# Attention scores as two stacked f32r products, with an f32r mask and separate buffers for even and odd heads

## The reference

```python
# fox: c is the running sum of the log forget gates
sc = einsum('bhqd,bhkd->bhqk', qb, k) * scale + (cb[..., :, None] - c[..., None, :])
sc = where(pos[None, :] <= tq[:, None], sc, -1e30); p = softmax(sc)
# diff: two maps c = 0, 1 for each head, one slope for each head
sc = einsum('bhcqd,bhckd->bhcqk', qb, k) * scale - slopes * (tq - pos)
p = softmax(where(pos <= tq, sc, -1e30)); a = p[:, :, 0] - lam * p[:, :, 1]
# na: 8 x 16 window clamped to the grid, bias rpb gathered by offset
sc = where(mask, einsum("bnqhd,bknjhd->bhnqkj", q_r, k_r) * scale + bias, NEG); p = softmax(sc)
```

## Time and profile before

| | us |
|---|---|
| median of three runs | 1433.59 (1426.29 to 1436.23) |
| the profiled execution's own time | 1433.59 |
| its span | 1431.8 |
| TensorE matmul busy | 1399.9 (98%) |
| TensorE weight load busy | 1137.6 |
| VectorE busy | 678.7 |
| ScalarE busy | 597.4 |
| GpSimd busy | 664.9 |

### The profile page before, as it was taken

How to read it: one execution, slowest core, us unless ns; L and a number is a source line. 1 busy time by engine, 2 the same in 40 slices (tenths; PEclk the granted TensorE clock), 3 DMA queues, 4 the chain that set the end, 5 groups by cost and what they waited for, 6 DMA issues and landing times.

```text
span 1431.8 us, 19476 instructions
## 1 busy us (share of the span) xinstructions
PE 1399.9 (98%) x6620; PEld 1137.6 (79%) x6620; DVE 678.7 (47%) x1228; ACT 597.4 (42%) x924; POOL 664.9 (46%) x886
## 2 busy tenths in 40 slices
PE   7999999999999999999998999999999999999998
PEld 5877787667888888888888777887778888888887
DVE  5566645555322222112277878666536555552111
ACT  5444433354544443334343554535335444443223
POOL 5422242215755545555545323455646545555551
PEclk9999999889999999999999999999999999999999
DMA  4321121112333333333364211332333333332331
GB/s 143 81 59 45 43 63 59 44 30 74 93 112 89 101 98 93 92 96 96 105 101 102 80 45 45 89 103 74 89 89 113 93 102 88 102 93 87 105 98 59
DMA packets 223632, 120.72 MB, mean 84 GB/s; under 512 B 15172, under 2 KB 222417, under 8 KB 223569
## 3 DMA queue, kind: packets, MB, share of 16 engines
q1 hardware_dynamic: 223569, 119.89, 29.7%
HBM read 117.56 MB, written 2.31 MB: 84 GB/s over the span
## 4 chain that ended last, share of the span: by engine, by line
PE 92%; DVE 3%; issue 1%; POOL 1%; ACT 1%; DMA 1%; SPq 1%; DVEq 0%; POOLq 0%; ACTq 0%
PE PS L677 28%; PE PS L679 27%; PE PS L678 27%; PE PS L827 2%; PE PS L838 2%; PE PS L855 2%; PE PS L828 1%; PE PS L829 1%; POOL WL L552 1%; DVE XL L1501 1%; DVE SS L1497 1%; PE PS L832 1%; DMA ROWV<-in_diff_norm_g 0%; PE PS L840 0%; SPq L451 0%
## 5 line engine op out<-in xcount | busy, mean ns | idle before, releaser
L552 POOL TENSOR_TENSOR WL<-RAW,WH 128x256 fp32r<-128x256 f32 x864 | 659.2, 795 | 735.5 <-ACT WH L1089 735.3
L677 PE MATMUL PS<-XH,WH 128*128 128x512 f32 x1088 | 434.9, 400 | 3.2 <-DVE X L1826 1.8
L679 PE MATMUL PS<-XH,WL 128*128 128x512 f32 x1088 | 425.2, 391 | 0.0
L678 PE MATMUL PS<-XL,WH 128*128 128x512 f32 x1088 | 424.6, 390 | 0.0
L1089 ACT ACTIVATE WH<-RAW 128x1024 fp32r<-128x1024 f32 (+1 forms) x220 | 228.7, 1041 | 431.9 <-PE PS L679 375.7
L677 PEld LDWEIGHTS PS<-XH,WH 128*128 128x128 f32 x1088 | 205.7, 189 | 45.8 <-DVE X L1826 2.6
L679 PEld LDWEIGHTS PS<-XH,WL 128*128 128x128 f32 x1088 | 204.8, 188 | 43.5
L678 PEld LDWEIGHTS PS<-XL,WH 128*128 128x128 f32 x1088 | 205.0, 188 | 40.0 <-issue 0.7
L677 PE MATMUL PS<-HH,WH 128*128 128x512 f32 (+1 forms) x374 | 141.0, 377 | 0.0
L679 PE MATMUL PS<-HH,WL 128*128 128x512 f32 (+1 forms) x374 | 140.8, 377 | 0.0
L678 PE MATMUL PS<-HL,WH 128*128 128x512 f32 (+1 forms) x374 | 140.8, 377 | 0.0
(11 more groups left out here) (312 smaller groups left out, 1920.9 us busy)
## 6 DMA issues: line engine op xcount, KB each, us to landing
RAW<-in_w_up SPq DMA_DIRECT2D x66, 512.0 KB, 3.8
RAW<-in_w_in SPq DMA_DIRECT2D x60, 512.0 KB, 3.9
RAW<-in_w_down SPq DMA_DIRECT2D x32, 512.0 KB, 4.0
RAW<-in_w_gate SPq DMA_DIRECT2D x22, 512.0 KB, 3.8
RAW<-in_w_out SPq DMA_DIRECT2D x16, 512.0 KB, 3.7
RAW<-in_w_down SPq DMA_DIRECT2D x16, 384.0 KB, 3.4
XTM<-in_x SPq DMA_DIRECT2D x4, 512.0 KB, 6.4
RAW<-in_w_na_out SPq DMA_DIRECT2D x4, 512.0 KB, 3.4
```

What stands on the lines that cost most here:

```text
L552: ins = pool.tensor_tensor(WL[:, s, cs], RAW[:, s % 2, cs], WH[:, s, cs].bitcast(F32), ALU.subtract)
L677: pe.matmul(out, ah, bh, start=start, stop=False)
L678: pe.matmul(out, ah, bl, start=False, stop=False)
L679: return pe.matmul(out, al, bh, start=False, stop=stop)
```

## The change

The four score tiles become QA, QB, KA, KB with [128, 2, 512]: the second index is now the head's parity, and a head has all 128 rows. QA holds the head's high queries on its own half and its low queries on the other; KA its high keys on both halves. So QA x KA over 128 rows is high x high plus low x high. QB holds the high queries on the head's half, and on the other half zeros with two rows of ones; KB the low keys, and on the other half zeros with the two bias rows. So QB x KB is high x low plus bias. The causal mask is an f32r identity against [zeros | mask], always 256 columns wide. Na keeps its bf16 mask. A score is three matmuls in all three stages.

High parts (`head_part`, two ScalarE instructions of 64 rows for a head) and low parts (`head_low`, two on VectorE) are now made head by head at fixed steps (`HEAD_STEPS`). The copy of the high half to the other rows or tile goes by DMA (`head_rows`, on SP's queue, ahead of the load of a given weight unit, `HEADS_BEFORE`), and so do the bias rows; those of fox heads 0 and 1 are issued by ScalarE after `v_parts`. The Q and K fillers end up to one step earlier. In diff the order is four blocks of map 0, then four of map 1; the probabilities of map 0 are kept in one part of PR for all four blocks, and ScalarE scales them. Zeros and ones are set once (`plain_rows`: M1 at the start, M2 in the "cab" stage). At the start of na the ten convolution taps that follow each other 5 and 5 become 2, 2, 3, 3. The first gates' conversion waits for step 28.

```diff
-                    QH=..., QL=..., KH=..., KL=...   [P, 2, S]: second index is the pair's parity
+                    QA=..., QB=..., KA=..., KB=...   [P, 2, S]: second index is the head's parity
...
+            sc = [(hd, comp, qb) for hd in range(4) for comp in range(2) for qb in range(4)]
+            ready_after = {8 * hd + 4 + qb: 4 * hd + qb for hd in range(4) for qb in range(4)}
...
-        qk_steps = [(max(4 * f - 1, 0), 4 * f + 2) for f in range(8)]
+        qk_steps = [(0, 2), (3, 5)] + [(4 * f - 2, 4 * f + 1) for f in range(2, 8)]
...
-            order = [("qk", 0, 0, 2), ("qk", 1, 3, 6), ("qk", 2, 7, 9), ("qk", 3, 10, 12), ("oa", 0, 13, 13),
-                     ("oa", 1, 14, 14), ("qk", 4, 15, 18), ("qk", 5, 19, 22), ("oa", 2, 24, 26), ("oa", 3, 27, 29),
+            order = [("qk", 0, 0, 2), ("qk", 1, 3, 5), ("qk", 2, 6, 8), ("qk", 3, 9, 12), ("oa", 0, 13, 13),
+                     ("oa", 1, 14, 14), ("qk", 4, 15, 17), ("qk", 5, 18, 21), ("oa", 2, 23, 25), ("oa", 3, 26, 29),
...
+    HEAD_STEPS = {"fox": {5: [("fox", 2)], 8: [("fox", 3)], 13: [("fox", 4)], 16: [("fox", 5)], 21: [("fox", 6)],
+                          24: [("fox", 7)], 30: [("diff", 0)], 32: [("diff", 1)]},
+                  "diff": {5: [("diff", 2)], 8: [("diff", 3)], 12: [("diff", 4)], 16: [("diff", 5)], 21: [("diff", 6)],
+                           24: [("diff", 7)]},
+                  "na": {5: [("na", 2)], 8: [("na", 3)], 13: [("na", 4)], 16: [("na", 5)], 21: [("na", 6)],
+                         24: [("na", 7)]}}
+    EVEN_DONE = 28
+    HEADS_BEFORE = {}
+    for kind, first in (("fox", UN["foxf"] + 6), ("diff", UN["difff"] + 6), ("na", UN["naf"] + 6)):
+        for i, head in enumerate(range(2, 8)):
+            HEADS_BEFORE.setdefault(first + i, []).append((kind, head))
+    for head in range(2):
+        HEADS_BEFORE.setdefault(UN["difff"] + head, []).append(("diff", head))
+        HEADS_BEFORE.setdefault(UN["naf"], []).append(("na", head))
...
+        def head_rows(kind, head):
+            e, mem = head % 2, FAM[kind]["mem"]
+            nat, oth = half_rows(e), half_rows(1 - e)
+            sp.wait_ge(head_hi, 2 * (FAM[kind]["h0"] + head) + 2)
+            sp.dma_start(mem["QB"][nat, e, :].bitcast(F32), mem["QA"][nat, e, :].bitcast(F32)).then_inc(head_in[e], 16)
+            sp.dma_start(mem["KA"][oth, e, :].bitcast(F32), mem["KA"][nat, e, :].bitcast(F32)).then_inc(head_in[e], 16)
+            if kind == "diff" or (kind == "fox" and head >= 2):
+                dst, src = bias_rows_of(kind, head)
+                sp.dma_start(dst, src).then_inc(head_in[e], 16)
...
-                pe.matmul(out, mem["QH"][r, par, q], mem["KH"][r, par, ks], start=True, stop=False)
-                pe.matmul(out, mem["QH"][r, par, q], mem["KL"][r, par, ks], start=False, stop=False)
-                pe.matmul(out, mem["QL"][r, par, q], mem["KH"][r, par, ks], start=False, stop=False)
+                pe.matmul(out, mem["QA"][:, e, q], mem["KA"][:, e, ks], start=True, stop=False)
+                pe.matmul(out, mem["QB"][:, e, q], mem["KB"][:, e, ks], start=False, stop=False)
...
-                    pe.matmul(out, sel, CR[:, 0:wide], start=False, stop=False)
-                    ins = pe.matmul(PS[:, SCO + g % 2, n - P:n], IDB[:, :], CMB[:, :], start=False, stop=True)
+                    mask = CMR[:, :]
+                    if n == P:
+                        mask = bass.AP(tensor=mask.tensor, offset=CMR[:, P:P + 1].offset, ap=[list(mask.ap[0]), [0, 2], [1, P]])
+                    ins = pe.matmul(PS[:, SCO + g % 2, wide - 256:wide], IDR[:, :], mask, start=False, stop=True)
...
+            act.wait_ge(acc_free, ak + 1)
+            if kind != "na" and f["h0"] + head >= 2 or kind == "na" and head >= 2:
+                act.wait_ge(sc_ready, f["s0"] + 4 * (head - 1))
+                act.wait_ge(head_in[e], heads_in(kind, head) - 16 * (2 if kind == "na" else 3))
+            for name, a, bias in (("QA", aq, ...), ("KA", ak, ...)):
+                    ins = act.activation(f["mem"][name][r, e, :], tile_t(a)[r, :], ACT.Copy)
+                ins.then_inc(head_hi, 1)
...
         v_parts("v1", M1, 0, gate_logs)
+        act.wait_ge(cr_dve, 2)
+        for head in range(2):
+            dst, src = bias_rows_of("fox", head)
+            act.dma_start(dst, src).then_inc(head_in[head], 16)
...
+                for kind_, head in HEAD_STEPS[kind].get(i, []):
+                    head_part(kind_, head)
                 for it in fills_done(kind, i):
...
                     if it["ends"] and i < LAST_STEP:
                         hi_next(it["unit"])
...
         for i in range(2):
             qk_take("na0", i, RP[:, :])
-            qk_low("na0", i, 0, M2, 0)
-            conv_taps(5, n_early)
+            conv_taps(2, n_early)
+        for i in range(2):
+            head_low("na", i)
+            conv_taps(3, n_early)
```

More of the change, by code:

```diff
@@ new lines, in fills_done, with fill_chunks, gate_place, init_bank @@
+    def fills_done(kind, step):
+        return [it for it in fill_plan(kind) if it["s1"] == step]
+    def fill_chunks(it, step, n):
+        k = it["s1"] - it["s0"] + 1
+        i = step - it["s0"]
+        return range(n * i // k, n * (i + 1) // k)
+    def gate_place(c):
+        return KD + 2 * c if c < 4 else KD + 1 + 2 * (c - 4)
+    def init_bank(c):
+        return (3, 4, 5, 6, 7, 3, 4, 5)[c]
+    def out_bank(t, half):
+        return (3, 1, 4, 5)[t] if half else 4 + t
+    def early_bank(s):
+        return (ACC, ACC + 1, OB, OB + 1)[s]
@@ new lines, in keys_of, with pair_index, half_rows, head_tiles @@
+    def keys_of(kind, qb):
+        return NA_KEYS[qb] if kind == "na" else (0, qb + 1)
+    def pair_index(kind, hd):
+        return hd if kind == "diff" else hd // 2
+    def half_rows(e):
+        return slice(e * HD, e * HD + HD)
+    def head_tiles(kind, head):
+        pair = head // 2
+        if pair == 0:
+            a = {"fox": TL["fox0"], "diff": TL["foxf"] + 6, "na": TL["na0"]}[kind]
+            return a, a + 1
+        return tuple(it["a"] for it in fill_plan(kind) if it["what"] == "qk" and it["idx"] in (2 * pair - 2, 2 * pair - 1))
@@ L458, in _ @@
         load_units(4, 6)
+        for head in range(2):
+            head_rows("fox", head)
         sp.wait_ge(pool_made, 1)
@@ L571, in _ @@
         lo_down(marks["down2"])
[L576 to L587, removed]
@@ L809, in scores @@
                 g = s0 + i
[L810 to L812 removed]
+                head = i // 4
+                e = head % 2
+                if qb == 0:
+                    pe.wait_ge(head_lo, 2 * (f["h0"] + head) + 2)
+                    pe.wait_ge(head_in[e], heads_in(kind, head))
                 if g >= 2:
                     pe.wait_ge(exp_ready, g - 1)
[L815 to L817 removed]
                 k0, k1 = keys_of(kind, qb)
@@ L1469, in tile_ready, with heads_drained @@
                 dve.wait_ge(w_used, UN[name] + i + 1)
+        def heads_drained(a):
+            done = [f["h0"] + 2 * pair + 2 for kind, f in FAM.items() for pair in range(4)
+                    for t in head_tiles(kind, 2 * pair) if t < a and t % 4 == a % 4]
+            if done:
+                dve.wait_ge(head_lo, 2 * max(done))
         def slots_drained(name):
@@ L1618, in _ @@
             qk_take("fox0", i, R[:, :])
-        for i in range(2):
-            qk_low("fox0", i, 0, M1)
+        for head in range(2):
+            head_low("fox", head)
         dve.wait_ge(fl_ps, 1)
```

277 lines of the change are left out of this document (148 added, 129 removed).

## The result

The changed kernel takes **1416.26 us** (median; 1414.13 to 1416.90) beside 1433.48 us of the kernel before on the same chip: ratio 0.9888, 95% interval 0.9855 to 0.9921, so 17 us less. Forecast was 1397 us, 36 us less, with a range of 1387 to 1416. The profiled execution has a span of 1415.1 us.

What follows compares the result with a forecast made beforehand. The prediction took TensorE's instruction order to bound the three attention stages. A TensorE gain of 54.7 us less 18.3 us added gave net -36.4 us, from 1433.59 to 1397 us, range 1387 to 1416.

Steps and rivals of the forecast that it cites:

- What a score costs: Fox and diff scores on TensorE fall to 0.67, 0.77 and 0.89 us at 256, 384 and 512 columns.
- Rival C: 128-row products go at their weight loads' pace, 0.19 to 0.20 us instead of 0.12: 1411 us, chance 0.08.
- the overlap rule: Weight loads overlap running products only when row groups differ, so no score would get shorter: 1452 us; the prediction excluded it.
- Even heads' chain: From K filler to landed copies takes 5.3 us; fits fox's and na's 6.6, diff's head 2 waits 0.3 to 0.5.
- Rival A: Head copies of 128 KB land late, at 3.9 us, so even heads wait: 1413 us, chance 0.13.
- Diff, step 21: A weight load queued behind head 6's copies delays conversion and exp; TensorE stalls 6.7 us before step 24, +5.0 us.
- start of fox: Bias rows of heads 0 and 1, issued after the weight conversion, delay the first scores to 72.6 us: +4.7 us.
- start of na: Three convolution taps and two low parts on VectorE delay na's start: +3.0 us.
- VectorE: the step that failed: Allowance for VectorE's added load: 2.0 us in fox (0 to 6) and 2.0 in na (0 to 8).
- na's own gain: Cheaper scores and transposes on TensorE save 1.28 us a head in na, 10.2 us for eight heads.
- Rival B: VectorE becomes the bound; fox loses 6 and na 8 us: 1407 us, chance 0.10.
- Rivals D and E: D, waits bring half clock: 1476 us, chance 0.05; E, lost switches only move, gains cancel: 1434 us, chance 0.04.

Runs made afterwards that it cites:

- experiment 10: The changed kernel with fox's and diff's causal mask again one bf16 product over 128 columns: 1415.7 us, ratio 0.9884 to the kernel before.
- experiment 12: Changed kernel with repaired starts, fox's mask building moved out, taps replanned, diff's last K filler one step earlier and four na bias-row fetches first: 1391.8 us, ratio 0.9721.
- experiment 6: The changed kernel with the 18 steps that build na's masks moved out of fox, before and behind it: 1408.8 us, ratio 0.9846.
- experiment 3: The changed kernel with a head's two low parts behind the low probabilities in VectorE's step, in all three stages: 1413.9 us, ratio 0.9884.
- experiments 5: The changed kernel with fox's first bias rows issued before the weight conversions and diff's head 6 copied one load later: 1407.9 us, ratio 0.9836.

## Why the prediction was wrong, point by point

- **What a score costs: right.** 0.67, 0.79, 0.91 us where 0.67, 0.77, 0.89 stood. A head near fox's end takes 10.75 us instead of 13.2, with 10.4 forecast; 0.3 of the difference is PV, whose first product comes some 0.2 late and runs with 0.34 instead of 0.23 to its successor. With the masks out the heads take 10.75 and 11.15 us in turn, so a head of fox saves 2.05 to 2.45 us where 2.8 was forecast. Rival C (pace of the weight loads) is out: successors are 0.12 us apart at 256 columns, each with its own 128-row weight, whose load takes 0.19 to 0.20 us. The Trainium skill's page "TensorE: Matmul & The Clock Gate" has the overlap rule in its section "The mechanism" and not in the one that the prediction names, and the same section also lets a load run ahead that targets the background weight buffer. The rule as the prediction puts it is against this trace; with that second case it is not.
- **Where that gain comes from: half right.** From the score products of 64 rows and their selector product, not from the operand type of the mask (experiment 10).
- **Even heads' chain: right.** At heads 2, 4 and 6 of fox and na TensorE has no wait over 0.25 us that a copy ended. The 0.5 us that diff's head 2 was to wait did not come either. Rival A is out.
- **Diff, step 21: right** (6.4 for 6.7), **start of fox: right** (+4.8 for +5.5 with the low parts of V's start), **start of na: nearly** (+4.2 for +3.3), but for another reason: the wait is for weights that land in 7.6 us instead of 5.3, not for VectorE. Why they land later in the changed kernel than before, with the same transfers in the queue, stays open; experiment 12 shows that the bias-row fetches ahead of them make up the time.
- **Diff as a whole: 1.6 us better, by luck.** Its half clock lasted 10.2 us instead of 13.7, which is worth 1.7 us; the prediction had not counted on it.
- **VectorE: the step that failed.** "In fox ... I allow 2.0 us (0 to 6). In na ... 2.0 (0 to 8)." Measured: fox 4.4 (87.8 less 82.0 with the masks out, less the 1.4 of the stretch at fox's start), na 11.9 (106.0 less 94.1 with the taps out, with the half clock that its waits brought), beyond the 8 that it allowed at most. That is 16.3 instead of 4.0, and 12.3 of the 19 us that the prediction is off. I had compared VectorE's busy time with TensorE's new time (10.2 against 10.4 in fox, 96 against 105 in na), as if a queue could be filled to 90%. Here it could not: VectorE must wait for TensorE and ScalarE in turn (by 0.5 to 3.2 us, once or twice in nearly every head), and what it owes then comes late. In na 10.85 us of work made a head of 14.75 (13.4 at the full clock, in experiment 6), 8.34 us still one of 11.01 with 0.4 of waits. Of the 11.9 us, 3.4 are half clock: na has 10.2 us of it with the taps and 3.4 without, and a stretch costs half its length.
- **na's own gain: smaller by 5.0.** 10.2 forecast; with the taps out the distance fell by 5.2 (99.3 to 94.1). Of the missing 5.0 the wait at step 23, where TensorE has no filler, and its half clock are 2.8 + 1.7. The products are not to blame (0.28 saved on 384 columns).
- Rival B was the right one, with the wrong size: it had 14 us for VectorE at most and said 1407. Rivals D and E fell: of the attention stages na alone got new half-clock stretches, two of them with 10.2 us in all.

## What to carry to other kernels

When TensorE's instructions get cheaper, ask not whether the next engine's busy time fits under the new total, but whether it fits with the pauses that the hand-over forces on it at every tile: here VectorE's work at 76 or 77% of a head's time (9.29 of 12.04, 8.34 of 11.01, 8.12 of 10.75, 8.83 of 11.48) left TensorE waits of 0 to 0.7 us, and work nearly as long as TensorE's own (10.35 in fox, 10.85 in na) made heads of 12.15 and 13.4 to 14.75 us. Find that work's cheapest place with experiments in both kernels: moving it took 11 us off na after the change (8 off the whole kernel) and nothing before it. And undo each part of a change by itself: the f32r mask was no part of the gain.

## What the runs showed of the hardware

- A bf16 product between f32r ones over the same 128 rows cost its surroundings nothing: 0.67 us for the same stretch with either mask. Three products over 64 rows and one over 128 in the same place took 0.45 to 0.67 us more than two over 128 rows.
- A TensorE wait of 2.4 us or more in an attention stage came with a stretch at 1.2 GHz in all kernels looked at (2.46, 2.51, 2.77, 3.77, 4.87 and 6.41 us) but once (2.86 us at 829.7 us in experiment 3). One of 2.36 us did so in the changed kernel, and one of 2.36 or 2.37 did not in experiments 5 and 6. One of 1.64 and one of 1.72 us did before the change; waits up to 1.44 us did not. These are the cases seen, not a rule.
- A copy of 128 KB from SBUF to SBUF landed 2.3 to 2.4 us after its issue for 20 of 24 heads of the changed kernel, and after up to 4.15 us among weight loads.
